# Sparse attention of the prompt: unnormalised queries with their scale in the bias sum, two branches as one, and the compressed branch of all units in one stage

## What is computed

```python
def rms_norm(x, g):
    y = x * lax.rsqrt(jnp.mean(x * x, axis=-1, keepdims=True) + EPS)
    return y * g
...
q = rms_norm(q, nsa_g_q)                       # 12 heads of 128
kc = rms_norm(nsa_compress(rows[:, :, 0], ...), g_k[0])   # 8 compressed keys
vc = nsa_compress(rows[:, :, 1], ...)
s_c = einsum('blghd,bcgd->bghlc', qg, kc) * scale + bias_c
o_cmp = einsum(..., masked_softmax(s_c, dist_c >= 0), vc)
...
ks = rms_norm(rows[:, :, 2], g_k[1])           # selected branch
o_sel = masked_softmax(q ks * scale + group_bias(table, t5_bucket(dist))) vs
kw = rms_norm(win_k, g_k[2])                   # window branch
o_win = masked_softmax(q kw * scale + bias_w) vw
o = gt[:, :, 0] * o_cmp + gt[:, :, 1] * o_sel + gt[:, :, 2] * o_win
```

## Time and profile before

| | us |
|---|---|
| median of 3 runs | 3719.41 (3717.89 to 3720.55) |
| the profiled execution | 3719.51 |
| its span | 3717.7 |
| preparation from the first sum of squares, 687.7 to 730.3 | 42.6 |
| attention of the two groups, 730.3 to 890.9 | 160.6 |

### The profile page before, as it was taken

How to read it: one execution, slowest core, us unless ns; L and a number is a source line. 1 busy time by engine, 2 the same in 40 slices (tenths; PEclk the granted TensorE clock), 3 DMA queues, 4 the chain that set the end, 5 groups by cost and what they waited for, 6 DMA issues and landing times. The chain is left out here.

```text
span 3717.7 us, 57142 instructions
## 1 busy us (share of the span) xinstructions
PE 3293.9 (89%) x23887; PEld 3057.6 (82%) x23887; DVE 1627.0 (44%) x1871; ACT 1283.0 (35%) x1379; POOL 176.1 (5%) x114
## 2 busy tenths in 40 slices
PE   7799999676577999999999999976769999999999
PEld 5699999354334999999999999964359999999999
DVE  4543334444454454433443353435464443344433
ACT  3422223223355343322332333235123333333332
POOL 0000000000233000000000000013200000000000
PEclk9899999755677999999999999976779999999999
DMA  4555353401554545454554544501544454545454
GB/s 146 179 161 178 117 160 91 138 1 46 165 187 148 181 144 162 147 170 156 162 169 147 167 152 160 168 31 34 200 146 155 159 166 148 162 159 167 150 163 135
DMA packets 317205, 537.07 MB, mean 144 GB/s; under 512 B 18213, under 2 KB 115455, under 8 KB 316040
## 3 DMA queue, kind: packets, MB, share of 16 engines
q1 hardware_dynamic: 316376, 529.70, 44.0%
q10 hardware_dynamic: 624, 4.46, 0.3%
HBM read 517.23 MB, written 25.19 MB: 146 GB/s over the span
## 5 line engine op out<-in xcount | busy, mean ns | idle before, releaser
L469 DVE TENSOR_TENSOR project_weights_low<-ring,project_weights_high 128x2048 fp32r<-128x2048 f32 x344 | 788.5, 2292 | 1203.0 <-ACT project_weights_high L404 1203.0
L404 ACT ACTIVATE project_weights_high<-ring 128x2048 fp32r<-128x2048 f32 x344 | 658.6, 1915 | 1264.3 <-PE project_banks L334 1264.2
L332 PE MATMUL project_banks<-high,project_weights_high 128*128 128x288 f32 x2560 | 763.3, 298 | 45.0 <-DVE project_weights_low L459 41.1
L333 PE MATMUL project_banks<-low,project_weights_high 128*128 128x288 f32 x2560 | 761.3, 297 | 0.0
L334 PE MATMUL project_banks<-high,project_weights_low 128*128 128x288 f32 x2560 | 761.2, 297 | 0.0
L332 PE MATMUL project_banks<-up_high,project_weights_high 128*128 128x288 f32 x2048 | 609.8, 298 | 27.5 <-DVE project_weights_low L459 27.5
L333 PE MATMUL project_banks<-up_low,project_weights_high 128*128 128x288 f32 x2048 | 608.7, 297 | 0.0
L334 PE MATMUL project_banks<-up_high,project_weights_low 128*128 128x288 f32 x2048 | 608.5, 297 | 0.0
L332 PEld LDWEIGHTS project_banks<-high,project_weights_high 128*128 128x128 f32 x2560 | 488.2, 191 | 47.5 <-DVE project_weights_low L459 42.7
L333 PEld LDWEIGHTS project_banks<-low,project_weights_high 128*128 128x128 f32 x2560 | 487.8, 191 | 0.0
L334 PEld LDWEIGHTS project_banks<-high,project_weights_low 128*128 128x128 f32 x2560 | 486.5, 190 | 0.0
(11 more groups left out here) (477 smaller groups left out, 3187.5 us busy)
## 6 DMA issues: line engine op xcount, KB each, us to landing
ring<-in_w_up_dram SPq DMA_DIRECT2D x128, 1024.0 KB, 5.2
ring<-in_w_down_dram SPq DMA_DIRECT2D x128, 1024.0 KB, 5.1
ring<-in_gla_w_in_dram SPq DMA_DIRECT2D x40, 1024.0 KB, 5.1
h<-in_cache_nsa_kv_dram SPq DMA_DIRECT2D x256, 128.0 KB, 2.2
ring<-in_w_out_dram SPq DMA_DIRECT2D x32, 1024.0 KB, 5.1
ring<-in_nsa_w_in_dram SPq DMA_DIRECT2D x28, 1024.0 KB, 5.1
sp_keys_values<-in_cache_nsa_kv_dram SPq DMA_DIRECT2D x80, 256.0 KB, 3.6
ring<-in_w_mem_kv_dram SPq DMA_DIRECT2D x16, 1024.0 KB, 5.8
```

Of the source, the lines that this page charges most:

```text
L332: nc.tensor.matmul(bank, w_high, moving_high[:, kt], start=(kt == 0), stop=False)
L333: nc.tensor.matmul(bank, w_high, moving_low[:, kt], start=False, stop=False)
L404: nc.scalar.activation(weights_high[:, c % 2], g.ring[:, c % RING], ACT.Copy).then_inc(rounded, 1)
L469: nc.vector.tensor_tensor(weights_low[:, c % 2], g.ring[:, c % RING], weights_high[:, c % 2].bitcast(F32), ALU.subtract).then_inc(split, 1)
```

## The change

In `prepare_sparse` the 12 query tiles leave the rounds; two rounds of four tiles (keys, memory queries) are left. ACT squares all query columns at once into the idle weight ring; PE sums them with 24 matmuls that give one number per prompt query and one matmul for the sampled columns; the root and the reciprocal are taken once for all, and `q_scale` keeps the prompt's. Queries of the prompt stay unnormalised, and their gain goes into the keys. Three transfers copy the compressed values to three more groups of partitions.

`attend_sparse_prompt` replaces the two calls of `attend_prompt`. Selected and window branch are one operation with two rows of columns at each step, and the query's scale is multiplied in the sum with the bias. The compressed branch of all 24 units is calculated first, as one softmax over 192 columns, and put into `h`; the other branches are added to it. POOL scales the probabilities. There is one block and no loop over bodies. The diff, cut:

```diff
+            pe.wait_ge(few_read, 1)
+            pe.wait_ge(q_squared, 1)
+            for k in range(HEADS):
+                for i in range(QT):
+                    nc.tensor.matmul(rows_ps[:, 2, k * QT + i:k * QT + i + 1], q_squares[:, k, i * P:(i + 1) * P],
+                                     g.ones[:, 0:1], start=True, stop=True, skip_group_check=True)
+            nc.tensor.matmul(rows_ps[:, 3, 0:OWN_Q], g.ones[:], q_squares[:, :, SEQ:TOKENS], start=True, stop=True
+                             ).then_inc(q_summed, 1)
...
+            nc.scalar.activation(q_squares, g.p[:, 0:HEADS], ACT.Square).then_inc(q_squared, 1)
...
+            for j in range(1, 4):
+                sp.dma_start(g.cmp_v_prompt[32 * j:32 * j + CMP_PROMPT], g.cmp_v_prompt[0:CMP_PROMPT]
+                             ).then_inc(stored, 16)
...
+def attend_sparse_prompt(nc, g):
+    units = [(k, i) for k in range(HEADS) for i in range(QT)]
...
+        @block.gpsimd
+            for u in range(U):
+                pool.wait_ge(inverted, u + 1)
+                p = probs[:, u % 3, :, 0:width(u)]
+                nc.gpsimd.tensor_tensor(p, p, stat[:, u % 4, 2].unsqueeze(2).to_broadcast([P, 2, width(u)]), ALU.mult
+                                        ).then_inc(scaled, 1)
+        @block.tensor
...
+            for u, (k, i) in enumerate(units):
+                mm = nc.tensor.matmul(cmp_ps[:, 0, u * CMP_PROMPT:(u + 1) * CMP_PROMPT], g.p[:, k, i * P:(i + 1) * P],
+                                      g.cmp_k_prompt[:, k // HPG], start=True, stop=True, skip_group_check=True)
+            mm.then_inc(cmp_scored, 1)
+            scores(0)
+            scores(1)
+            pe.wait_ge(cmp_scaled, 1)
...
+            scores(2)
+            pe.wait_ge(cmp_copied, 1)
+            for n, (first, count) in enumerate(PASSES):
+                wait(pe, cmp_placed, n)
...
+            for u in range(U + 1):
+                if u < U:
+                    turn(u)
+                if u and u + 2 < U:
+                    scores(u + 2)
+                if u:
+                    if u == 1:
+                        pe.wait_ge(cmp_placed, len(PASSES))
+                    multiply(u - 1)
+        @block.vector
+            def front(u):
...
+                nc.vector.scalar_tensor_tensor(s[:, u % 2, :, 0:w], s_ps[:, u % 2, 0:2 * w].rearrange(
+                    "p (b k) -> p b k", b=2), g.q_scale[:, k, i:i + 1], bias, ALU.mult, ALU.add).then_inc(biased, 1)
...
+            for u in range(U):
+                if u + 2 < U:
+                    front(u + 2)
+                if u + 1 < U:
+                    back(u + 1)
+                if u:
+                    take(u - 1)
+            take(U - 1)
...
-                for h in range(GROUPS):
...
-                    attend_prompt(nc, g, f"sparse{h}", HPG // 2, 2,
...
+                attend_sparse_prompt(nc, g)
```

More of the change, by code:

```diff
@@ L1296, in _ @@
                     sums_ps[:, 0:FLIP_BANKS], ACT.Copy).then_inc(flip_copied, 1)
+            act.wait_ge(q_mean, 1)
+            nc.scalar.activation(q_rms[:], q_rms[:], ACT.Sqrt).then_inc(q_root, 1)
             for r in range(rounds):
@@ L1353, in _ @@
                     mean_square(r + 1)
-                if r + 2 < rounds:
-                    square(r + 2)
                 dve.wait_ge(spread_done, r + 1)
                 for o in range(BATCHED):
-                    t, gain, scale = normed[r * BATCHED + o]
-                    col = g.vec[:, gain:gain + 1] if scale == 1.0 else scaled_gain[:, int(gain == gm):int(gain == gm) + 1]
-                    if o == 0:
+                    tile, gain, scale = normed[r * BATCHED + o]
+                    if r == 0 and o == 0:
                         dve.wait_ge(turned, len(sets))
-                    last = nc.vector.scalar_tensor_tensor(g.p[:, t], g.p[:, t], col, sums_ps[:, o, 0:TOKENS], ALU.mult,
-                                                          ALU.mult)
+                    if gain == gm:
+                        parts = [(slice(0, TOKENS), scaled_gain[:, 1:2])]
+                    else:
+                        parts = [(slice(0, SEQ), key_gain[:, gain - gk:gain - gk + 1]),
+                                 (slice(SEQ, TOKENS), g.vec[:, gain:gain + 1])]
+                    for cols, col in parts:
+                        last = nc.vector.scalar_tensor_tensor(g.p[:, tile, cols], g.p[:, tile, cols], col,
+                                                              sums_ps[:, o, cols], ALU.mult, ALU.mult)
                 last.then_inc(scaled, 1)
@@ L3123, in sparse_layer @@
         g.cmp_v = sb("cmp_v", [P, BATCH, HD])
-        g.cmp_v_prompt = sb("cmp_v_prompt", [CMP_PROMPT, GROUPS, HD])
+        g.cmp_v_prompt = sb("cmp_v_prompt", [P, GROUPS, HD])
         with nc.sbuf_tensor(
@@ L3141, in sparse_layer @@
                     nc.sbuf_tensor("near", [P, HEADS, T_COLS], F32) as near, \
-                    nc.sbuf_tensor("gates_prompt", [P, QT, gates], F32) as gates_prompt:
+                    nc.sbuf_tensor("gates_prompt", [P, QT, gates], F32) as gates_prompt, \
+                    nc.sbuf_tensor("q_scale", [P, HEADS, QT], F32) as q_scale:
+                g.q_scale = q_scale
                 g.rows, g.near, g.gates_prompt = rows, near, gates_prompt
                 prepare_sparse(nc, g, a)
-                for h in range(GROUPS):
[L3146 to L3155, removed]
-                    attend_prompt(nc, g, f"sparse{h}", HPG // 2, 2,
-                                  lambda m, k: p[:, bass.ds(head(m, k), 1), 0:SEQ].squeeze(1), branches,
-                                  lambda m, k, i: gates_prompt[:, i, bass.ds(head(m, k), BRANCHES, step=HEADS)],
-                                  lambda m, k, i: g.h[:, bass.ds(head(m, k), 1), i * P:(i + 1) * P].squeeze(1))
+                attend_sparse_prompt(nc, g)
             attend_memory_prompt(nc, g, 0, p, MEM_Q)
```

189 lines of the change are left out of this document (186 added, 3 removed).

## The result

The changed kernel took 3674.6 us in the median of four runs (3671.7 to 3680.3), the kernel before 3718.7 us beside it (3715.5 to 3720.6): a ratio of 0.9884, 95% interval 0.9867 to 0.9901. That is 44 us saved where the forecast gains add up to 31.9. The profiled executions are 47.8 us apart (spans of 3717.7 and 3669.9 us), since the one of the changed kernel is the fastest of its four; stages are compared between these two.

What follows compares the result with a forecast made beforehand. The prediction took loops of waits between engines, with no engine full, to bound the kernel. 3719.5 less 10.3 (preparation) and 21.6 (attention) gave 3687.6, stated as 3688 us; the range was 3658 to 3704.

Steps and rivals of the forecast that it cites:

- The chain of waits: Attention units: each link is turning over, scores, front and back, POOL; one unit long since back queues behind front.
- I take the loop at about 0.6: Granted clock assumed for the 24-unit attention loop, giving 28 + 107 + 4 = 139 us for the stage.
- Preparation: Tail of the preparation: last reciprocal 22.4 us after the first sum, before 32.7; gain 10.3 us, bounds 7.5 and 13.5.
- The 24 sums: Preparation, sums over query squares on PE: 10.3 us at the low clock, 5.2 at the high, taken as 8.0.
- Opening: Compressed scores, softmax and outputs ahead of the units: 30.7 us at the low clock, 19 with PE's terms halved, taken as 28.
- The link: Attention loop, one unit's turning over to the next: mean 5.14 us at the low clock, 4.17 at the high.
- the 160.6 taken: Time of the two old attention blocks, 80.3 us each, from which the forecast 139 us were subtracted: gain 21.6 us.
- the rising clock: Rival, attention stage: the clock rises and stays, stage 112 us, total 3659 us; chance 0.20.
- Three units in flight: Rival, attention loop: three probability buffers hide the loop, PE bounds at about 3.5 us a unit, total 3664; chance 0.06.
- the short gain: Rival: opening overlaps nothing, first units fill behind it (another 7 us), preparation gains only 7.5; total 3700; chance 0.12.
- POOL in the loop: Rival: POOL products at 2.3 us, not 0.9, cost 31 us and lose the loop's gain; 3723 at 2.5 us; chance 0.06.

Runs made afterwards that it cites:

- the first experiment: Changed kernel with DVE issuing back of unit u+1 ahead of front of unit u+2 instead of behind it: 3652.2 us, ratio to before 0.9823.
- the run with copies first: Changed kernel with back ahead of front on DVE, plus ACT's copies of turned probabilities ahead of its exponentials: 3646.1 us, ratio 0.9805.

## Why the prediction was right, and where its sizes were off

The forecast gain was 31.9 us; the trace shows 47.8 and the medians 44, both inside the stated range, which is wide because it spans the two clocks. The chain of waits came out as described. The term furthest off is "I take the loop at about 0.6", for this trace; two others were mis-sized.

- **Preparation: right.** The last reciprocal starts 711.73 - 689.58 = 22.15 us after the first sum; 22.4 were worked out. The 24 sums took 7.0 us for 8.0. The forecast 10.3 us are 72.0 - 61.5 = 10.5 against the run with the old preparation, and 10.9 by the tail alone (42.6 to 31.7). In the pair of profiles only 8.0 remain, since PE reached the first sum 2.9 us later after the stage's start than in before. The start and the first flips, before:

```profile
660.86 6.53 PE L1232 MATMUL prep_rows_ps<-ident,projected 128*128 128x128 f32 x36 [0.62 <-PEq L850]
...
673.17 4.25 PE L1256 MATMUL prep_sums_ps<-near,sparse_masks 128*128 128x512 f32 x6
```

and after:

```profile
659.83 5.38 PE L1239 MATMUL prep_rows_ps<-ident,projected 128*128 128x128 f32 x36 [0.62 <-PEq L850]
...
673.78 5.49 PE L1263 MATMUL prep_sums_ps<-near,sparse_masks 128*128 128x512 f32 x6
```

That is clock: from the gate rows to the end of these flips PE was busy throughout in both, for 6.33 us at 0.73 before and for 8.90 us at 0.50 after, which is 2.6 of the 2.9 us. The run with the old preparation also has 5.49 us for the flips and reaches the first sum 29.7 us after the stage's start, as the changed kernel does (29.8), so the new instructions are not the cause. Why the one profile of before got the higher clock there stays open.
- **Opening: 28 us taken, 22.9 measured.** Scores (10.4), six transposes (1.5) and the waits were as worked out at the low clock, and the burst did not bring the high one (0.50 over the whole opening). But the output matmuls take 2.1 and 1.2 us for 7.2 and 3.7: I multiplied a single duration by a count where neighbours run side by side. The 30.7 us of the sum at the low clock less these 7.6 are 23.1.
- **The link: right to 0.1 us** at both clocks. POOL took 0.61 and 1.04 us for 0.70 and 1.10, which is 0.08 us a link, some 2 us in all. That the loop is one unit long, and through which order, the first experiment shows.
- **The loop's clock: the largest miss.** It was 0.77 in the profiled run. By the two link means the step from 0.6 to 0.77 is 0.99 x 0.17/0.5 = 0.34 us a link, 7.4 us in 22. Loop and end took 100.6 us for 111; with POOL's 2 us that leaves 1 us unexplained. The value is not one that the code fixes: 0.77, 0.75, 0.73, 0.67 and 0.61 came up with the same loop, so 0.6 was at the low end of what it gets, and the size of this miss is in part the luck of the execution that was profiled. The second profile of the changed kernel, at 0.67, is 4.4 us longer over twenty links.
- **The rest** is 1.0 us ahead of the preparation, 1.3 us in the memory attention and -0.1 us behind it, which are not the change's own, and 0.5 us by which the two old blocks were longer than the 160.6 taken.

Sum: 31.9 - 2.3 + 5.1 + 10.4 + 1.0 + 1.3 - 0.1 + 0.5 = 47.8.

Of the rivals, the rising clock came half true. That idle time brings the lower clock fits the loop, where extra matmuls gave 1.00 in place of 0.61 to 0.77; it does not by itself account for the gapless scores above, in which the clock fell. Three units in flight did not come true (no mean link near 3.5 us until the order was changed), nor did the short gain, as the opening did overlap the first units. POOL in the loop costs 7 us, far from the 31 that would have undone the gain.

## What to carry to other kernels

Write down, for every engine, the order in which the calls of neighbouring units are issued, and follow one unit round it: a call that needs nothing new but is queued behind one that waits sets the length of the loop, and swapping two lines was worth half of what the whole change brought. Forecast a stage that waits in turns at both clock levels and let the range span them, since the same code may get either. Before a matmul's duration is multiplied by a count, ask which partitions neighbours use.

## What the runs showed of the hardware that was not expected

- The granted clock of one unaltered loop was 0.77 in one execution and 0.67 in another, which is 4.4 us over twenty links. With an idle matmul in the waits it was 1.00 and the runs agreed to 0.3 us.
- In a run of eight-column score matmuls without a gap (7.69 us, after 2.04 us of idle time) the clock fell from 1.00 to 0.50; in the changed kernel the same matmuls had 0.50 throughout, where PE had stood idle for 3.76 us before them.
- Matmuls on eight rows in four groups of 32 partitions followed each other every 0.13 us on average (sixteen in 2.1), although each lasts 0.42.
- POOL's product of 256 and 512 columns takes 0.612 and 1.039 us in the mean, with a least value of 0.612 and a longest of 1.040 over all 24 units.
- In the run with copies first a DVE operation on two columns took 0.22 us beside such a product and 0.17 without it; one that reads 256 columns from PSUM took 0.48 us either way.
